# Two modulation chunks of the first MLP summed in the first blocks of the sparse attention, their gate rows formed in block 8

## The reference, cut to what matters

```python
mod = (c_act @ ada_w[layer] + ada_b[layer])[:, None, :]
sh_a, sc_a, gt_a, sh_m, sc_m, gt_m = jnp.split(mod, 6, axis=-1)
h = modulate(rms_norm(x, attn_norm[layer]), sh_a, sc_a)
...                                    # mix: layer 0 differential, layer 1 sparse attention
x = x + gt_a * mix
h = modulate(rms_norm(x, mlp_norm[layer]), sh_m, sc_m)
x = x + gt_m * squared_relu_mlp(h, mlp_w1[layer], mlp_w2[layer])
```

## Time and profile before

| | |
|---|---|
| median of 3 runs (lowest, highest) | 1310.14 us (1309.81, 1311.36) |
| the profiled execution: its time, its span | 1312.58 us, 1310.8 us |
| PE, PEld, DVE, ACT, POOL busy | 96%, 84%, 66%, 53%, 10% of the span |
| mean DMA rate over the span | 204 GB/s |

### The profile page before, as it was taken

The page is one execution under the profiler, slowest core; times in us unless marked ns, Lnnn a source line. Parts: engine busy times, 40 slices in busy tenths (PEclk is TensorE's granted clock), DMA queues, the critical chain, the costliest instruction groups (busy, mean ns, idle before and its releaser), DMA issues.

```text
span 1310.8 us, 21652 instructions
## 1 busy us (share of the span) xinstructions
PE 1262.0 (96%) x8368; PEld 1095.4 (84%) x8368; DVE 860.9 (66%) x1501; ACT 691.7 (53%) x1219; POOL 137.1 (10%) x154
## 2 busy tenths in 40 slices
PE   7999899999999999999999989999999999999999
PEld 5887799888799656899898867999998778899997
DVE  6588699997675675786546774665565566654444
ACT  3566553444455665645445874644444565654542
POOL 1022111211100000101100320100100100010100
PEclk9999999999999999999999999999999999999999
DMA  9979379999489142585553532685554554466550
GB/s 366 388 240 346 120 274 353 356 352 347 137 244 288 50 177 65 184 319 181 191 172 108 176 94 81 158 315 183 172 181 141 176 178 137 154 184 198 179 161 33
DMA packets 123781, 267.38 MB, mean 204 GB/s; under 512 B 11040, under 2 KB 33824, under 8 KB 123296
## 3 DMA queue, kind: packets, MB, share of 16 engines
q1 hardware_dynamic: 119328, 257.23, 59.2%
q0 software_dynamic: 1728, 6.29, 1.5%
q10 hardware_dynamic: 2624, 2.49, 0.6%
HBM read 264.83 MB, written 1.15 MB: 203 GB/s over the span
## 4 chain that ended last, share of the span: by engine, by line
PE 63%; DVE 5%; ACT 3%; issue 2%; POOL 1%; DVEq 0%; ACTq 0%; POOLq 0%
PE bank L538 12%; PE bank L540 11%; PE bank L539 11%; PE ps_s L538 3%; PE ps_s L539 3%; PE ps_s L540 3%; PE ps_p L539 3%; PE ps_p L538 3%; PE ps_p L540 3%; PE ps_s L1326 1%; DVE wlo L1621 1%; PE ps_p L1169 1%; PE ps_p L1145 1%; POOL rs L3446 1%; PE ps_s L1133 1%
## 5 line engine op out<-in xcount | busy, mean ns | idle before, releaser
L1621 DVE TENSOR_TENSOR wlo<-wring,whi 128x1024 fp32r<-128x1024 f32 (+1 forms) x376 | 457.9, 1227 | 265.4 <-ACT whi L2767 261.0
L2767 ACT ACTIVATE whi<-wring 128x1024 fp32r<-128x1024 f32 (+1 forms) x376 | 388.3, 1045 | 364.0 <-PE bank L540 132.2
L538 PE MATMUL bank<-h_hi,whi 128*128 128x256 f32 (+1 forms) x1224 | 348.8, 285 | 5.7 <-DVE wlo L1621 2.6
L539 PE MATMUL bank<-h_lo,whi 128*128 128x256 f32 (+1 forms) x1224 | 346.2, 283 | 0.0
L540 PE MATMUL bank<-h_hi,wlo 128*128 128x256 f32 (+1 forms) x1224 | 346.1, 283 | 0.0
L538 PEld LDWEIGHTS bank<-h_hi,whi 128*128 128x128 f32 (+1 forms) x1224 | 234.0, 191 | 11.9 <-issue 10.1
L539 PEld LDWEIGHTS bank<-h_lo,whi 128*128 128x128 f32 (+1 forms) x1224 | 234.1, 191 | 0.8
L540 PEld LDWEIGHTS bank<-h_hi,wlo 128*128 128x128 f32 (+1 forms) x1224 | 234.1, 191 | 0.0
L3462 POOL TENSOR_TENSOR ex<-ex 128x512 f32<-128x512 f32 x64 | 82.1, 1285 | 670.7 <-ACT g_hi L2898 670.5
L538 PE MATMUL ps_s<-whi,g_hi 128*128 128x512 f32 x256 | 101.2, 395 | 2.5 <-DVE wlo L1621 2.5
L538 PE MATMUL ps_p<-whi,g_hi 128*128 128x512 f32 x256 | 100.5, 393 | 0.0
(11 more groups left out here) (391 smaller groups left out, 1773.5 us busy)
## 6 DMA issues: line engine op xcount, KB each, us to landing
wring<-in_mlp_w SPq DMA_DIRECT2D x128, 512.0 KB, 5.3
wring<-in_mlp_w_in SPq DMA_DIRECT2D x64, 512.0 KB, 3.8
wring<-in_mlp_w_out SPq DMA_DIRECT2D x64, 512.0 KB, 4.1
wring<-in_ada_w_t SPq DMA_DIRECT2D x48, 512.0 KB, 8.0
wring<-in_ada_w SPq DMA_DIRECT2D x36, 512.0 KB, 5.8
wring<-in_moba_w_qkv SPq DMA_DIRECT2D x24, 512.0 KB, 4.0
wring<-in_a_qk SPq DMA_DIRECT2D x16, 512.0 KB, 9.2
wring<-in_kv_ada_w_t SPq DMA_DIRECT2D x16, 512.0 KB, 7.4
```

Of the source, the lines that this page charges most:

```text
L538: nc.tensor.matmul(out, lh, rh, start=first, stop=False, skip_group_check=mixed)
L539: nc.tensor.matmul(out, lh, rl, start=False, stop=False, skip_group_check=mixed)
L1621: v.tensor_tensor(piece_view(wlo, p), raw_view(p), piece_view(whi, p).bitcast(F32), ALU.subtract).then_inc(lo_ready, 1)
L2767: a.activation(piece_view(whi, p), raw_view(p), ACT.Copy).then_inc(hi_ready, 1)
```

## The change

Chunks 4 and 5 of layer 1 leave the first MLP. Their eight matvecs go into DVE's blocks 0 (two) and 1 to 6 (one each), behind `nsa_weigh` and ahead of `nsa_low`. Their loads go between those of `b_out` and of chunks 8 and 9. PE's gate rows move from block 2 to block 8, DVE's copies of them from block 4 to block 8. The list `drain_order`, from which waits on finished chunks are counted, is changed to fit.

```diff
-    plan += mix(mlp("m0"), ada(0, range(10, 12)) + ada("kv", range(4)) + ada(1, range(6)))
+    plan += mix(mlp("m0"), ada(0, range(10, 12)) + ada("kv", range(4)) + ada(1, range(4)))
...
-    for tag, lo, hi in (("b_out", 0, 2), ("b_out_mid", 2, 3), ("b_out_end", 3, 4)):
-        plan += [((tag, c[0][1]),) + c[1:4] + (c[4][lo:hi],) for c in b_out]
-        plan += ada_by_rows(1, range(8, 10)) if lo == 0 else []
+    gate_parts = [c[:4] + (c[4][j:j + 1],) for c in ada(1, range(4, 6)) for j in range(4)]
+    row_halves = [c[:4] + (c[4][j:j + 2],) for c in ada_by_rows(1, range(8, 10)) for j in (0, 2)]
+    out_part = {(tag, c[0][1]): [((tag, c[0][1]),) + c[1:4] + (c[4][lo:hi],)] for c in b_out
+                for tag, lo, hi in (("b_out", 0, 2), ("b_out_mid", 2, 3), ("b_out_end", 3, 4))}
+    plan += gate_parts[:2] + out_part["b_out", 0] + gate_parts[2:4]
+    for i in range(4):
+        plan += row_halves[i:i + 1] + (out_part["b_out", 1] if i == 3 else []) + gate_parts[4 + i:5 + i]
+    plan += [c for tag in ("b_out_mid", "b_out_end") for i in range(2) for c in out_part[tag, i]]
...
-                if b == 2:
+                if b == 8:
                     gate_rows("n1", 64 + 16)
...
-            mlp("m0", ada_order[10:22], last=lambda: (gate("m0"), gate_use("m0")))
+            mlp("m0", ada_order[10:20], last=lambda: (gate("m0"), gate_use("m0")))
...
+                for n in range(b + (b > 0), b + 2 if b < 7 else 0):
+                    matvec(ada_order[20 + n // 4], n % 4)
                 if b >= 4 and b % 2 == 0:
                     nsa_low((b - 4) // 2)
-                if b == 4:
+                if b == 8:
                     gate("n1")
```

More of the change, by code:

```diff
@@ L438, in build @@
         matvec_order = [ada_order[c] for c in CHUNKS] + ada_order[10:22] + ada_order[26:28]
-        drain_order = [ada_order[c] for c in opening + CHUNKS[:2] + ROWS[:1] + CHUNKS[2:] + ROWS[1:]] + ada_order[10:]
+        drain_order = [ada_order[c] for c in opening + CHUNKS[:2] + ROWS[:1] + CHUNKS[2:] + ROWS[1:]] + ada_order[10:20]
+        drain_order += ada_order[22:24] + ada_order[20:22] + ada_order[24:]
         def drained_by(*chunks):
```

## The result

The changed kernel takes 1322.58 us (median of 4 runs, 1320.68 to 1325.09) against 1309.97 us for the kernel before (4 runs beside them, 1308.57 to 1311.36): 12.6 us more, a ratio of 1.0098 with a 95% interval of 1.0077 to 1.0119. Predicted were 1316.1 us and a range of 1310.0 to 1320.5. The sign was right and the size was not: of +12.6 us the forecast had +6.0. Ratios are taken over runs at a like granted clock; one run of the study, 1551.49 us at a mean clock of 0.75, with the copies ahead, is left out.

The account below looks back on a forecast made before the run. PE was taken as the bound, busy 1262.0 of 1310.8 us. Terms -4.8 + 0.1 + 5.5 + 1.1 + 1.7 + 0.9 + 1.5 = +6.0 us, less 2.4 us left with the profiler, gave 1316.1 us, range 1310 to 1320.5.

Parts of the forecast that it names:

- Part 1: First MLP: without the eight loads and matvecs, PE's waits for weights go; 4.8 us saved, bounds 3.9 to 5.9.
- Part 2: Blocks 0 to 4: matvecs mostly fit DVE's idle times, gate rows' time comes back; +0.1 us, bounds -0.3 to +1.2.
- Part 3: Blocks 4 and 5: ACT waits for late b_out,1 loads, delaying PE's second turn; +5.5 us, bounds +3.1 to +8.4.
- part 4: Block 6: matvec n7 ahead of `nsa_low` makes PE's mix of step 4 late; +1.1 us, bounds 0 to 1.3.
- Part 6: After PE's idle time in block 5 the clock falls to its lower level; +1.5 us, bounds 0 to 1.7.
- 5, gate rows, copies: Block 8: PE pays 1.7 us for gate rows (0 to 1.95), DVE's copies show 0.9 us (0 to 1.3).
- The prediction's own sign of being wrong: No ACT wait on `in_b_w_out` over 2 us, or an MLP gain under 3 or over 6 us.
- Rival (a): Block 5's wait is short, loads landing 3.8 us after issue, and the MLP gain large; 1310.4 or 1309.3 us, chance 0.17.
- rival (d): ACT's wait covers PE's `nsa_low` delay, and gate rows fill PE's idle time in block 8; 1313.3 us, chance 0.17.
- Rival (b): DVE bounds blocks 0 to 6, six matvecs each delaying PE by half their length, 3.8 more; 1320 us, chance 0.13.
- Rival (c): The first MLP gives back only 1.0 us, its excess coming from DVE, not loads; 1320 us, chance 0.03.

Follow-up runs that it names:

- the copies ahead: Changed kernel with the two b_out,1 loads earlier in the list and block 8's gate copies ahead of `nsa_low`; 1312.71 us, ratio 1.0026.
- the relief alone: Kernel before without loads and matvecs of chunks 4 and 5 anywhere, zeros instead; 1309.1 us, ratio 0.9989.
- the second profile: The kernel before, unchanged, profiled once more in one run; 1308.38 us.
- The kernel with PE kept busy: Changed kernel plus 22 unused matmuls on constants in PE's block 5, ahead of the turn that waits for ACT; 1320.93 us, ratio 1.0083.
- the loads early: Changed kernel with the two b_out,1 loads at places 212 and 213 instead of 218 and 219; 1314.48 us, ratio 1.0040.

## Why the prediction was right in sign and wrong in size

The terms, forecast against what the runs show (us):

| part | forecast | measured | from |
|---|---|---|---|
| 1, relief of the MLP | -4.8 (-3.9 to -5.9) | -1.4 (-3.3 to +0.4) | runs of the relief alone |
| 2, matvecs to block 4 | +0.1 | +0.6, +0.8; 0.0 with the clock up | its two traces; three others |
| 3, ACT's wait | +5.5 | +6.0, +6.3 | its two traces |
| 4 and 6, `nsa_low` and the clock | +1.1 +1.5 | +4.7, +4.8 | its two traces |
| 5, gate rows, copies | +1.7 +0.9 | +1.8 +0.9 | five traces |
| sum, with the first value of each | +6.0 | +12.6 | runs: +12.6 |

The last two sums agree to the tenth by luck: the first term alone is uncertain by 1.9 us.

**Part 1 failed, by size, and it is half of the miss.** The mechanism "the removed loads cost PE its waits" was read from the earlier trace rows, the stretch of 26.31 us with its wait of 1.95. In two other executions with the same loads and matvecs in the MLP that stretch took 22.57 and 22.72 us. The DMA share is 0.94 to 0.99 in these stretches of all three, and a wait of ACT of 5 us and more need not reach PE: behind the 5.77 us of the second profile PE was busy without a gap. The bounds I gave, 3.9 to 5.9, asked only how much of that one excess would go, not whether it comes back each time. There was a hint: the profiled execution lay 2.4 us above the median of the runs, and I set that down to the profiler, though it could as well be an unusual stretch inside it. Later profiles of the kernel before and of its near variants lay at or below their medians (1308.38 against 1309.7). What slowed that first execution's loads stays open. The prediction's own sign of being wrong, an MLP that gains under 3 or over 6 us, came up both ways: 7.19 us against the first profile, 1.4 by the runs.

**Part 3 was right.** With T at 450.39 - 5.39 = 445.0 in the changed kernel, the second load was there at 452.5, T + 7.5 where T + 7.0 stood, and 454.63 - 453.62 = 1.01 us led from the split to the turn (forecast 1.07). The order of the queue was the cause: with the same work and only the list changed, the wait was gone. Rival (a), a short wait, is out: 6.2 us to landing, not 3.8.

**Part 6 failed, by size, and it covered part 4.** I took the 3.60 us stretch behind a 1.95 us wait for the longest the low clock would last, and its 1.7 us for the upper bound. Behind a wait three times as long it lasted 13.7 us, in both executions, though PE was busy all the time from 456 to 464 us. The kernel with PE kept busy shows it to cost 4.6 us in the ten behind the turn. At the mix of step 4 PE then comes later than DVE and has no wait (the row at 469.11), so n7 ahead of `nsa_low` doesn't show; with the clock up it shows in full, 1.16 us. The two terms don't add: 4.7 together, against 2.6. The Trainium skill, "TensorE: Matmul & The Clock Gate", section "HAM oscillation — how this bites in real kernels", prices low time at half its length (1 - 1.2/2.4). By that rule the estimate is 13.7 / 2 = 6.8 us for the whole stretch. The trace has 4.7: some 2.3 us of the low time had passed when PE's wait ended at 454.63, and 0.54 us went into a wait for DVE that PE had in block 7 before. The estimate and the trace are both far above the bound of 1.7.

**Parts 2 and 5 and the direction were right.** Part 2's +0.1 held where the clock stayed up; the low stretch at 432 us, which the prediction didn't have, makes the difference. The gate rows' 1.7 us show in every trace that has them, the copies' 0.9 in every one that has them behind `nsa_low`, and nothing behind gives them back, against rival (d), whose other half, part 4 hidden behind what comes before it, came true. Rival (b), DVE as the bound of blocks 0 to 6, is out: the offset stays at -5.39 us from block 3 to the wait. Rival (c) had the size of part 1 nearly right, 1.0 us, for another reason: it blamed DVE for the excess, and the excess was not there. It had 0.03, and deserved more: the price of a rare event stands in no row of one trace.

## What to carry to other kernels

Here the stretch where the DMA queues were full was the one that a single profile misjudged: hold the length of such a stretch against a second execution, or bound its gain below by zero when the profiled run lies above the median. Read the mean granted clock of all runs beside their times: a few tenths of a per cent of it are some us here, more than most terms of the sum. A list of loads is an order of waits: before moving a load, find which buffer the ones ahead of it wait for, since a queue in order hands that wait to data that had a free buffer. And a long wait of PE cost itself and the clock after it, and what hid behind the low clock came out when the clock was mended.

## What the runs showed of the hardware

- The clock's low stretch was longer behind the longer wait: 0.54 over 3.6 us behind 1.95 us, 13.7 us at 1.2 GHz behind 5.91 and 6.21 us. Why it outlasts so much busy time isn't settled here.
- The same small waits of 0.55 and 1.08 us in block 7 went with a lower clock (0.77, 0.81) in the kernel with PE kept busy and with none in the two traces with the loads early and n7 ahead.
- A wait of PE of 1.65 us between 521 and 537 us stands in all ten traces. Behind it the clock fell (0.72 over the 6 us from 526 in the row above) in three, and stayed 1.00 in the other seven. Whether the clock falls behind a given short wait varies from trace to trace, and so do the runs of one kernel (1312.17 to 1317.71 with the loads early).
- Two 512 KB loads issued in one row, right behind a third, had landed 6.2 us after issue in the median, as the third of three did before.
